# A gated block kernel's first mixer: position columns as a third group of the compression's product, and gelu, gate and clamps with one operand in PSUM

## The chip, the cores and the metric

The kernel runs on one core of one Trainium2 chip. The metric is the device time of one execution in microseconds (us). The core has a matrix engine (TensorE, in the rows PE, its weight loads PEld), a vector engine (VectorE, DVE), a scalar engine (ScalarE, ACT), GpSimd (POOL) and a queue that issues the DMAs (SyncE, SP). SBUF is the memory beside the engines; PSUM holds what the matrix engine writes and can be read and written by DVE and ACT.

## The reference, cut to what matters

Two blocks of two layers each are run over 256 tokens of width 1024. Each layer is a mixer and a gated feed-forward part. Only the first mixer is touched here. It projects the normed input and runs a retention of four heads and a sparse attention with three branches beside each other:

```python
proj = (h @ w_in).astype(jnp.float32)
(rq, rk, rv, rg, nq, kc, vc, ks, vs, kw, vw, ng) = _split(proj, EVEN_SIZES)
...
o_r = retention_chunkwise(q_r, k_r, heads(rv, RET_HEADS))
mu = jnp.mean(o_r, axis=-1, keepdims=True)
var = jnp.mean(jnp.square(o_r - mu), axis=-1, keepdims=True)
o_r = (o_r - mu) * lax.rsqrt(var + 1e-5)
o_r = ... * jax.nn.silu(rg)                      # the retention's gate
...
k_cmp = nsa_compress(kvh(kc), pos_k, w1_k, w2_k)  # and the same for v
...
def nsa_compress(kv, pos_emb, w1, w2):
    # 15 blocks of 32 tokens with a step of 16, two groups
    flat = (blocks + pos_emb.astype(jnp.float32)).reshape(B, G, n, CMP_BLOCK * d)
    return jax.nn.gelu(flat @ w1.astype(jnp.float32)) @ w2.astype(jnp.float32)
```

Since `(blocks + pos) @ w1 = blocks @ w1 + pos @ w1`, the kernel takes the product of the positions by itself, as one column that is the same for every block, and adds it. The attention's compressed branch has only 15 keys; its softmax keeps rows without a valid key at zero with small clamps.

## The kernel before

**Units.** All large products are a stream of weight chunks of up to 128x1024 elements. SP loads a chunk into `raw`, ACT rounds it into `whi` (line 1913, `split`), POOL takes the rest into `wlo` (line 2180, `lo`), and TensorE multiplies: for each 128 rows of weights the two products with `whi` (lines 1037 and 1038) and one with `wlo` (line 1044). Six chunks can be ahead: chunk c is rounded once chunk c-6 is used up. One chunk for one half of the tokens (t = 0 or 1) is a unit (`product`). The first mixer has units 0 to 69: seven blocks of projection columns (block 2 is 280 wide with units 16 to 21, the others 512 wide with eight units; the last, block 6, is the retention's gate and ends with unit 53), and from unit 54 on the output projection, whose units alternate t = 0, 1 up to 61. A block's product lies in `G[0]`, 512 columns for each t; `evict` (EV) copies it to `PJ0` with the norm's scale.

**Steps.** Everything else is small steps, each named by two letters and a key, and the order on every engine is written out by hand in `PLAN`: line "18:" lists the steps that come after unit 18, and each engine takes from it those that are its own, in that order. Engines are in order, so a step that waits holds everything behind it on its engine. Steps wait for each other by semaphores counted by `nth`.

**The compression.** TT turns the keys and values, TC (ACT, lines 2005 and 2006) copies them into `Z`, one plane of 256 columns for each of two groups, the lower 64 rows shifted by a token. CA (TensorE) then makes 16 matmuls over 30 columns (two groups of 15 blocks, line 1113), and 16 with one column, the positions held in `CP` (line 1117), with the same weights `w1c`. In the rows each such matmul of 32-bit floats stands as two. CB (DVE) copies the position's column to SBUF, adds it and makes the argument of gelu's exponential; CE (ACT) is the exponential; CD (DVE) finishes gelu; CF (TensorE) is the second product and CG (DVE) copies it to `CK`.

**The attention.** For branch br (0 compressed, 1 selected, 2 window), group g and half t: SC scores (TensorE, line 1146), MK mask and maximum (DVE), EX exponentials (ACT), TR turned weights (TensorE, line 1182), CPA and CPV their copies (ACT, DVE), AV weighted values (TensorE, line 1211), NO gated sum into `MX` (DVE). They work in three lanes: `@0` and `@1` are PSUM tiles A0 and A1, `@2` is `G[1]`; a lane's next user waits until the one before has finished.

**The retention's gate.** R1 to R7 make the retention's heads, their mean and the inverse deviation, in lane 2 (heads 0 and 1, key 0) and lane 0 (heads 2 and 3, key 1). After EV 6 t, GS (DVE, line 1683) clamps the negated gate from `PJ0` into the compression's old weights `w1c`, GT (ACT, lines 1902, 1904 and 1906) makes its sigmoid there, GU (DVE, line 1689) multiplies it into the gate in `PJ0`, and R8 (DVE, lines 1667 and 1675) normalises four 128x128 pieces in PSUM and writes their product with the gate to `MX`. MT 2 (TensorE, line 1080) turns key 0 of it, MH and ML (ACT, DVE) round it, MT 3 does so for key 1; the output projection needs MH/ML 2 from unit 62 and MH/ML 3 from unit 64 on.

## Time and profile before

| | |
|---|---|
| median of 3 runs | 1376.7 us (1375.18 to 1377.59) |
| the profiled execution's own time | 1377.06 us |
| its span, first to last instruction | 1375.3 us |
| TensorE busy | 1330.7 us, 97% of the span |
| POOL, ACT, DVE busy | 1033.3, 717.1 and 383.5 us |
| mean granted TensorE clock | 0.984 of full |

The profile is of one execution. Its own time lies 0.36 us over the median and 1.8 us over its span. Busy time of an engine says little by itself: what matters is which waits lie on the chain of work that ended last. Matmuls are pipelined, so the durations of neighbours overlap; the starts tell the pace. A granted clock of 1.00 is 2.4 GHz and 0.50 is 1.2 GHz.

### The profile page before, as it was taken

How to read it: one execution, taken by the hardware profiler on the slowest of the kernel's cores; microseconds unless marked ns; L12 is line 12 of the kernel's file. 1: busy time of each engine (PE TensorE's matmuls, PEld its weight loads, DVE VectorE, ACT ScalarE, POOL GpSimd, SP SyncE). 2: the span in 40 equal slices, each digit the busy share in tenths (PEclk: the TensorE clock that was granted, in tenths of full speed). 3: DMA queues.
4: the chain of work that ended last, by engine and by line, in shares of the span. 5: the costliest groups of instructions: out<-in, count | busy, mean ns of one | idle time of the engine just before them, and what ended most of it. 6: DMA issues, size and time to landing. Idle time of an engine off the chain costs nothing.

```text
span 1375.3 us, 19563 instructions
## 1 busy us (share of the span) xinstructions
PE 1330.7 (97%) x7558; PEld 1095.0 (80%) x7558; DVE 383.5 (28%) x812; ACT 717.1 (52%) x1259; POOL 1033.3 (75%) x875
## 2 busy tenths in 40 slices
PE   6999999999999999999999998999999999999997
PEld 4888788888878777888887777788887788788886
DVE  1155421111157653110104463301103232411112
ACT  6355564454478776544444664444534554544431
POOL 6354878887885467888888776788879877788874
PEclk9799999999999999999999999999999999999999
DMA  8232456665644244666665643566656545466652
GB/s 272 92 108 77 138 172 184 188 196 172 193 158 124 79 123 128 201 190 183 180 191 158 184 125 122 154 214 186 196 173 209 182 140 153 139 214 187 197 170 89
DMA packets 63117, 224.92 MB, mean 164 GB/s; under 512 B 7345, under 2 KB 7985, under 8 KB 63025
## 3 DMA queue, kind: packets, MB, share of 16 engines
q1 hardware_dynamic: 62736, 223.57, 53.2%
q8 instruction: 60, 0.98, 0.3%
q14 instruction: 33, 0.26, 0.1%
q10 hardware_dynamic: 288, 0.10, 0.0%
HBM read 222.59 MB, written 1.05 MB: 163 GB/s over the span
## 4 chain that ended last, share of the span: by engine, by line
PE 88%; DVE 3%; POOL 3%; ACT 3%; DMA 2%; issue 2%; DVEq 0%; SPq 0%; ACTq 0%
PE G L1037 25%; PE G L1044 25%; PE G L1038 25%; POOL wlo L2180 3%; PE A L1211 2%; PE A L1068 1%; ACT whi L1913 1%; PE A L1146 1%; PE G L1211 1%; PE A L1182 1%; PE A L1058 1%; PE A L1080 1%; DMA raw<-in_w_e 0%; DMA raw<-in_w_a 0%; PE A L1320 0%
## 5 line engine op out<-in xcount | busy, mean ns | idle before, releaser
L2180 POOL TENSOR_TENSOR wlo<-raw,whi 128x256 fp32r<-128x256 f32 (+1 forms) x867 | 1023.7, 1218 | 324.0 <-ACT whi L1913 323.9
L1913 ACT ACTIVATE whi<-raw 128x1024 fp32r<-128x1024 f32 x403 | 425.1, 1060 | 357.3 <-PE G L1044 334.4
L1037 PE MATMUL G<-whi,xh 128*128 128x512 f32 (+2 forms) x1200 | 464.9, 391 | 9.2 <-DVE xl L1392 6.8
L1038 PE MATMUL G<-whi,xl 128*128 128x512 f32 (+2 forms) x1200 | 452.0, 380 | 0.0
L1044 PE MATMUL G<-wlo,xh 128*128 128x512 f32 (+2 forms) x1200 | 353.2, 380 | 1.3 <-POOL wlo L2180 1.3
L1037 PEld LDWEIGHTS G<-whi,xh 128*128 128x128 f32 x1200 | 228.3, 190 | 52.2 <-ACT whi L1913 7.6
L1038 PEld LDWEIGHTS G<-whi,xl 128*128 128x128 f32 x1200 | 228.6, 190 | 37.7
L1044 PEld LDWEIGHTS G<-wlo,xh 128*128 128x128 f32 x1200 | 219.9, 190 | 46.6 <-POOL wlo L2180 3.2
L1037 PE MATMUL G<-whi,hh 128*128 128x512 f32 x352 | 139.4, 396 | 0.0
L1038 PE MATMUL G<-whi,hl 128*128 128x512 f32 x352 | 138.8, 394 | 0.0
L1044 PE MATMUL G<-wlo,hh 128*128 128x512 f32 x352 | 110.4, 395 | 0.0
L1044 PEld LDWEIGHTS G<-wlo,hh 128*128 128x128 f32 x352 | 66.3, 188 | 15.4
L1038 PEld LDWEIGHTS G<-whi,hl 128*128 128x128 f32 x352 | 66.3, 188 | 15.1
L1037 PEld LDWEIGHTS G<-whi,hh 128*128 128x128 f32 x352 | 66.4, 189 | 15.0
L1431 DVE SCALAR_TENSOR_TENSOR sa<-G,SM,sa 128x512 f32<-128x512 f32 (+1 forms) x24 | 16.9, 706 | 165.5 <-PE G L1044 165.5
L1434 DVE TENSOR_TENSOR sa<-G,sa 128x512 f32<-128x512 f32 (+1 forms) x24 | 15.5, 646 | 169.7 <-PE G L1044 169.7
L1442 DVE TENSOR_TENSOR hl<-A,hh 128x512 fp32r<-128x512 f32 (+1 forms) x48 | 31.1, 647 | 96.0 <-ACT hh L1982 96.0
L1037 PE MATMUL G<-whi,mh 128*128 128x512 f32 x128 | 53.5, 418 | 2.4 <-DVE ml L1449 1.5
L1038 PE MATMUL G<-whi,ml 128*128 128x512 f32 x128 | 51.6, 403 | 0.0
L1375 DVE SCALAR_TENSOR_TENSOR G<-X,G 128x512 f32<-128x512 f32 x16 | 11.1, 696 | 119.3 <-PE G L1044 119.3
L1375 DVE SCALAR_TENSOR_TENSOR X<-X,G 128x512 f32<-128x512 f32 x16 | 11.0, 687 | 114.8 <-PE G L1044 114.8
L1044 PE MATMUL G<-wlo,mh 128*128 128x512 f32 x128 | 41.5, 406 | 0.0
(340 smaller groups left out, 1196.7 us busy)
## 6 DMA issues: line engine op xcount, KB each, us to landing
raw<-in_g SPq DMA_DIRECT2D x88, 512.0 KB, 3.9
raw<-in_u SPq DMA_DIRECT2D x88, 512.0 KB, 4.0
raw<-in_d SPq DMA_DIRECT2D x88, 512.0 KB, 4.2
raw<-in_w_h SPq DMA_DIRECT2D x32, 512.0 KB, 3.6
raw<-in_w_e SPq DMA_DIRECT2D x24, 512.0 KB, 3.7
raw<-in_w_a SPq DMA_DIRECT2D x24, 512.0 KB, 3.6
raw<-in_w_b SPq DMA_DIRECT2D x24, 512.0 KB, 3.8
raw<-in_w_eo SPq DMA_DIRECT2D x8, 512.0 KB, 3.6
```

The costliest lines, as they stand in the source:

```text
L1037: e.matmul(o, sh[:, kt, xs], whi[h][:, ws], start=u.first and j == 0, stop=False)
L1038: e.matmul(o, sl[:, kt, xs], whi[h][:, ws], start=False, stop=False)
L1044: m = e.matmul(o, sh[:, kt, xs], wlo[h][:, ws], start=False, stop=u.stop and final)
L1058: m = e.transpose(A[t][:, 512 * b + 128 * i:512 * b + 128 * i + 128], X[:, t, 512 * b + 128 * i:512 * b + 128 * i + 128], ident)
L1068: m = e.transpose(A[t][:, 512 * (b % 2) + 128 * i:512 * (b % 2) + 128 * i + 128], sa[b % 2][:, t, 128 * i:128 * i + 128], ident)
L1211: m = e.matmul(tile[:, ow * i:ow * i + ow], w[1][0:kp, at:at + 128], vs[i][b], start=b == 0, stop=b == nb - 1)
L1375: e.scalar_tensor_tensor(out=x if st < 4 else ps, in0=x, scalar=1.0 if st < 4 else ALPHA, in1=ps, op0=ALU.mult, op1=ALU.add).then_inc(S["R ...
L1431: e.scalar_tensor_tensor(out=s_, in0=ps, scalar=rstd[st - 1, t], in1=s_, op0=ALU.mult, op1=ALU.mult).then_inc(S["HM"], 1)
L1434: e.tensor_tensor(s_, ps, s_, ALU.mult).then_inc(S["HM"], 1)
L1442: e.tensor_tensor(hl[sl], ps, hh[sl].bitcast(F), ALU.subtract).then_inc(S["HL"], 1)
L1913: e.activation(whi[c % NH][:, 0:n], raw[c % NR][:, 0:n], ACT.Copy).then_inc(s_hi, 1)
L2180: m = e.tensor_tensor(wlo[c % NH][:, i:j], raw[c % NR][:, i:j], whi[c % NH][:, i:j].bitcast(F), ALU.subtract)
```

## The change

It has five parts. (1) `Z` has a third plane for each of keys and values; MB, at the start, clears it and copies the 16 position columns into its even places, and CA becomes 16 matmuls over 45 columns (30 in use before, now three groups of 15); the 16 one-column matmuls are gone, and column 30 of the result is the position's. (2) Gelu's intermediates u and v lie in the lane's PSUM tile. (3) GS reads the gate's product from `G[0]` with the norm's scale instead of the evicted copy; TensorE's first unit of the output projection for each t now waits for GS as well as EV, since it writes `G[0]`. GU is gone; R8 makes two products over 512 columns, heads by sigmoid in PSUM and that by the gate in `PJ0` into `MX`. (4) The compressed branch's mask, maximum and clamps, NO's clamp and the copy in R6 are done in PSUM or left out. (5) The plan's lines 17 to 47 and 53 to 57 are in another order. Parts of the diff that repeat these are left out.

```diff
-17: TC 0; SC 1 0 0 @2; TC 1; CA 0 @0; MK 1 0 0; EX 1 0 0; CA 1 @1; CB 0; CE 0; TR 1 0 0; CD 0
-18: CPA 1 0 0; CB 1; CF 0; EV 2 0; AV 1 0 0; CG 0; CE 1
-19: CD 1; CF 1; SC 1 0 1 @0; CG 1; SC 0 0 0 @1; MK 1 0 1
+17: TC 0; SC 1 0 0 @2; TC 1; CA 0 @0; MK 1 0 0; EX 1 0 0; CA 1 @1; CB 0; CE 0; CD 0; TR 1 0 0
+18: CB 1; CPA 1 0 0; CF 0; EV 2 0; AV 1 0 0; CG 0; CE 1; SC 1 0 1 @0; CD 1; CF 1
+19: MK 1 0 1
+20: CG 1; SC 0 0 0 @1; EX 1 0 1
 21: MK 0 0 0
-22: EV 2 1; EX 1 0 1; GD
-24: GE; EX 0 0 0; TR 1 0 1; NO 1 0 0
-25: CPA 1 0 1; CPV 1 0 1; TT 3 @2; RO 0 0; AV 1 0 1; TC 3; SC 2 0 0 @2; NO 1 0 1; TR 0 0 0
...
+30: EX 0 0 1; TR 2 0 1; NO 2 0 0
+31: CPV 2 0 1; CPA 2 0 1; TR 0 0 1; SC 1 1 0 @2; AV 2 0 1; CPA 0 0 1; MK 1 1 0; EX 1 1 0; AV 0 0 1; NO 2 0 1
+32: NO 0 0 1; TR 1 1 0; SC 1 1 1 @0; CPA 1 1 0; MT 0 @1; MK 1 1 1; AV 1 1 0; MH 0
...
+40: NO 0 1 0; R1 0 @2
+41: MK 0 1 1; R2A 0; R2V 0; EX 0 1 1; R1 1 @0; R3 0; R2V 1; EV 5 0; TR 0 1 1; R2A 1; R4 0
+42: CPA 0 1 1; AV 0 1 1; R3 1; NO 0 1 1
+43: R4 1; MT 1 @1
...
+46: EV 5 1; R5 0; R5 1; R6 0
+47: R6 1; R7 0
 48: R7 1
 50: EV 6 0; GS 0
 51: GT 0
-53: GU 0
-54: EV 6 1
-55: GS 1; GT 1
-57: GU 1; R8 0; R8 1; MT 2 @1
+54: EV 6 1; GS 1
+55: GT 1
+56: R8 0
+57: R8 1; MT 2 @1
...
-        Z = sb("Z", [128, 4, 256], F, e0)
+        Z = sb("Z", [128, 6, 256], F, e0)
...
@@ -1025,6 +1026,8 @@
                         e.wait_ge(S["EV"], nth("EV", u.st, u.blk - 1, u.t))
                     elif u.st % 2 == 0 and wide and u.bank == 0:
                         e.wait_ge(S["EV"], nth("EV", u.st, len(BLOCKS[u.st]) - 1, u.t))
+                        if u.st == 0:
+                            e.wait_ge(S["GS"], nth("GS", 0, u.t))
...
-                e.wait_ge(d_cp, 16)
+                e.wait_ge(S["MB"], nth("MB", 0))
                 for m in range(16):
-                    z = Z[:, 2 * kind:2 * kind + 2, 2 * m:2 * m + 225:16]
+                    z = Z[:, 3 * kind:3 * kind + 3, 2 * m:2 * m + 225:16]
                     wt = w1c[:, kind, 64 * m:64 * m + 64]
-                    e.matmul(tile[0:64, 0:30].rearrange("p (g i) -> p g i", g=2), wt, z, start=m == 0, stop=m == 15)
-                for m in range(16):
-                    wt = w1c[:, kind, 64 * m:64 * m + 64]
-                    pos = CP[:, (POSV if kind else POSK) + m:(POSV if kind else POSK) + m + 1]
-                    o = e.matmul(tile[0:64, 512:513], wt, pos, start=m == 0, stop=m == 15)
+                    o = e.matmul(tile[0:64, 0:45].rearrange("p (g i) -> p g i", g=3), wt, z, start=m == 0, stop=m == 15)
                 o.then_inc(S["CA"], 1)
...
-                x, u, bias = w[0][0:64, 0:30], w[0][0:64, 32:62], w[0][0:64, 96:97]
+                x, u, bias = w[0][0:64, 0:30], tile[0:64, 64:94], w[0][0:64, 96:97]
                 k = -2.0 * (2.0 / np.pi) ** 0.5
                 e.wait_ge(S["CA"], nth("CA", *key))
-                e.tensor_copy(bias, tile[0:64, 512:513]).then_inc(s_dve, dv.up())
...
-                _, w = lane_of("CA", key)
-                x, u, v = w[0][0:64, 0:30], w[0][0:64, 32:62], w[0][0:64, 64:94]
+                tile, w = lane_of("CA", key)
+                x, u, v = w[0][0:64, 0:30], tile[0:64, 64:94], tile[0:64, 96:126]
                 e.wait_ge(S["CE"], nth("CE", *key))
                 e.tensor_scalar(u, u, 1.0, None, ALU.add).then_inc(s_dve, dv.up())
                 own()
                 e.reciprocal(v, u).then_inc(s_dve, dv.up())
                 own()
-                e.tensor_tensor(x, x, v, ALU.mult).then_inc(S["CD"], 1)
...
+                else:
+                    e.wait_ge(d_cp, 16)
+                    e.memset(Z[:, 2:6:3, :], 0.0).then_inc(s_dve, dv.up())
+                    own()
+                    for kind, at_pos in enumerate((POSK, POSV)):
+                        e.tensor_copy(Z[:, 3 * kind + 2, 0:32:2], CP[:, at_pos:at_pos + 16])
                 e.tensor_copy(one[:, :], ident)
                 e.tensor_copy(under[:, :], CN[:, at + 128:at + 256]).then_inc(S["MB"], 1)
...
                     e.wait_ge(d_cn, 16)
-                    mask = CN[:, C_CMP + 16 * t:C_CMP + 16 * t + nk].unsqueeze(1).to_broadcast([128, 2, nk])
-                    for b in range(2):
-                        m = e.tensor_tensor(s[:, b:4:2, :], heads4(tile[:, 512 * b:512 * b + 512], 2)[:, :, 0:nk], mask,
-                                            ALU.add)
-                    m.then_inc(s_dve, dv.up())
+                    mask = CN[:, C_CMP + 16 * t:C_CMP + 16 * t + nk].unsqueeze(1).to_broadcast([128, 4, nk])
+                    four = tile[:, :].rearrange("p (b k) -> p b k", b=4)[:, :, 0:nk]
+                    top = tile[:, 128:132]
+                    e.tensor_tensor(four, four, mask, ALU.add).then_inc(s_dve, dv.up())
                     own()
-                    e.tensor_reduce(mx[key], s, X_AX, ALU.max).then_inc(s_dve, dv.up())
+                    e.tensor_reduce(top.rearrange("p (i b) -> p b i", b=2),
+                                    tile[:, :].rearrange("p (b i k) -> p b i k", b=2, i=2)[:, :, :, 0:nk], X_AX, ALU.max,
+                                    ).then_inc(s_dve, dv.up())
                     own()
-                    e.tensor_scalar(mx[key], mx[key], -1.0e20, -1.0, ALU.max, ALU.mult).then_inc(S["MK"], 1)
+                    e.tensor_scalar(mx[key], top, -1.0e20, -1.0, ALU.max, ALU.mult).then_inc(S["MK"], 1)
...
+                    e.tensor_scalar(over, sm[key], 1.0e-30, None, ALU.max).then_inc(s_dve, dv.up())
                     own()
-                e.reciprocal(over, sm[key]).then_inc(s_dve, dv.up())
+                e.reciprocal(over, over if br == 0 else sm[key]).then_inc(s_dve, dv.up())
...
-                m.then_inc(s_dve, dv.up())
-                own()
-                e.tensor_copy(ret_va[hp], mv[:, 1:8:2]).then_inc(S["R6"], 1)
+                m.then_inc(S["R6"], 1)
...
+                heads = tile[:, :].rearrange("p (i b) -> p i b", i=2)[:, :, 0:256].rearrange("p i (t c) -> p i t c", t=2)
+                gate = w1c[:, :, 256 * hp:256 * hp + 256].rearrange("p t (i c) -> p i t c", i=2)
+                raw_gate = PJ0[:, :, RG + 256 * hp:RG + 256 * hp + 256].rearrange("p t (i c) -> p i t c", i=2)
+                to = MX[:, :, 512 + 256 * hp:768 + 256 * hp].rearrange("p t (i c) -> p i t c", i=2)
...
                 for t in range(2):
-                    e.wait_ge(S["GU"], nth("GU", 0, t))
-                for j in range(4):
-                    c, t, o = 128 * (2 * hp + j // 2), j % 2, 512 * (j // 2) + 128 * (j % 2)
-                    m = e.tensor_tensor(MX[:, t, 512 + c:640 + c], tile[:, o:o + 128],
-                                        PJ0[:, t, RG + c:RG + c + 128], ALU.mult)
-                m.then_inc(S["R8"], 1)
+                    e.wait_ge(S["GT"], nth("GT", 0, t))
+                    e.wait_ge(S["EV"], nth("EV", 0, 6, t))
+                e.tensor_tensor(heads, heads, gate, ALU.mult).then_inc(s_dve, dv.up())
+                own()
+                e.tensor_tensor(to, heads, raw_gate, ALU.mult).then_inc(S["R8"], 1)
 
             def ret_gate_clamp(key):
                 _, t = key
                 e.wait_ge(S["CA"], 2)
                 e.wait_ge(S["EV"], nth("EV", 0, 6, t))
-                e.tensor_scalar(w1c[:, t, 0:512], PJ0[:, t, RG:RG + 512], -1.0, 80.0, ALU.mult,
-                                ALU.min).then_inc(S["GS"], 1)
-
-            def ret_gate_silu(key):
-                _, t = key
-                e.wait_ge(S["GT"], nth("GT", *key))
-                e.tensor_tensor(PJ0[:, t, RG:RG + 512], PJ0[:, t, RG:RG + 512], w1c[:, t, 0:512],
-                                ALU.mult).then_inc(S["GU"], 1)
+                e.tensor_scalar(w1c[:, t, 0:512], G[0][:, 512 * t:512 * t + 512], rstd[-1, t], -80.0, ALU.mult,
+                                ALU.max).then_inc(S["GS"], 1)
...
+            def sigmoid_of_clamped(ap, done, sign=1.0):
+
+                e.activation(ap, ap, ACT.Exp, scale=sign).then_inc(s_act, ac.up())
...
-                        e.activation(Z[0:64, 2 * k + g, :], src, ACT.Copy)
-                        m = e.activation(Z[64:128, 2 * k + g, 0:255], src[:, 1:256], ACT.Copy)
+                        e.activation(Z[0:64, 3 * k + g, :], src, ACT.Copy)
+                        m = e.activation(Z[64:128, 3 * k + g, 0:255], src[:, 1:256], ACT.Copy)
...
-                _, w = lane_of("CA", key)
-                u = w[0][0:64, 32:62]
+                tile, _ = lane_of("CA", key)
+                u = tile[0:64, 64:94]
...
-                    m = e.activation(ps if key[0] == 4 else s[:, i, :], s[:, i, :] if key[:2] == (0, 0) else ps, ACT.Exp,
+                    m = e.activation(ps if key[0] == 4 else s[:, i, :], ps, ACT.Exp,
...
-                rstd_of(ret_r[hp], ret_va[hp], 1, 1.0, S["R7"])
+                rstd_of(ret_r[hp], ret_mv[hp][:, 1:8:2], 1, 1.0, S["R7"])
...
-                sigmoid_of_clamped(w1c[:, key[1], 0:512], S["GT"])
+                sigmoid_of_clamped(w1c[:, key[1], 0:512], S["GT"], -1.0)
```

## Rows read from the trace of the kernel before

**Rows 1.** Page, parts 1, 2 and 4: busy time, granted clock, chain that ended last.

```profile
PE 1330.7 (97%) x7558; PEld 1095.0 (80%) x7558; DVE 383.5 (28%) x812; ACT 717.1 (52%) x1259; POOL 1033.3 (75%) x875
...
PEclk9799999999999999999999999999999999999999
...
PE 88%; DVE 3%; POOL 3%; ACT 3%; DMA 2%; issue 2%; DVEq 0%; SPq 0%; ACTq 0%
```

**Rows 2.** Busy time by window: busy us per engine (instructions), then granted clock, DMA share, GB/s.

```profile
49.18:54.50 5.32, 5.32 (x93) 5.32 (x92) 1.81 (x7) 2.55 (x12) 2.12 (x4) 1.00 0.63 200
...
54.86:58.41 3.55, 3.55 (x36) 3.54 (x35) 0.53 (x3) 0.00 (x0) 0.00 (x0) 0.50 0.00 0
58.41:68.25 9.84, 9.84 (x44) 8.38 (x45) 2.22 (x11) 2.26 (x4) 1.49 (x3) 0.50 0.01 2
...
70.88:154.88 84.00, 84.00 (x530) 70.15 (x528) 42.76 (x120) 47.91 (x136) 43.41 (x62) 1.00 0.32 95
```

**Rows 3.** Chain of waits through the compression: start, us, what.

```profile
49.25 1.99 PE A L1113 x32
51.24 1.84 PE A L1117 x32
...
55.11 3.37 PE A L1117 x32
58.48 1.04 PE G L1182 x4
```

**Rows 4.** The same chain, one weight row of an output unit, at either clock.

```profile
166.64 0.83 PE G L1044 x2
...
168.83 0.47 PE G L1044 x2
```

**Rows 5.** Timeline around gelu's argument and first scores, DVE.

```profile
53.11 0.15 DVE L1457 COPY W<-A 64x1 f32<-64x1 f32 x1 [3.12 <-PE A L1117]
...
55.27 0.18 DVE L1478 TENSOR_TENSOR W<-W 64x30 f32<-64x30 f32 x1
```

**Rows 6.** Timeline, ACT, end of the first exponentials.

```profile
51.50 0.21 ACT L2028 ACTIVATION_READ_ACCUMULATOR W<-G,SM 128x1 f32 x1
```

**Rows 7.** Timeline of DVE through the retention's gate.

```profile
148.93 0.43 DVE L1683 TENSOR_SCALAR w1c<-PJ 128x512 f32<-128x512 f32 x1 [3.47 <-ACT PJ L1926]
...
155.87 1.03 DVE L1683 TENSOR_SCALAR w1c<-PJ 128x512 f32<-128x512 f32 x1 [2.61 <-ACT PJ L1926]
158.93 1.22 DVE L1689 TENSOR_TENSOR PJ<-PJ,w1c 128x512 f32<-128x512 f32 x1 [2.02 <-ACT w1c L1906]
160.07 1.37 DVE L1667 TENSOR_SCALAR G<-G,SM 128x128 f32<-128x128 f32 x4
```

**Rows 8.** Timeline of ACT there.

```profile
155.09 0.67 ACT L1926 ACTIVATE PJ<-G,SM 128x512 f32<-128x512 f32 x1
...
158.26 0.63 ACT L1906 ACTIVATE w1c<-w1c 128x512 f32<-128x512 f32 x1
```

**Rows 9.** Timeline of PE there, idle time before in brackets.

```profile
155.81 0.50 PE L1037 MATMUL G<-whi,mh 128*128 128x512 f32 x1 [0.93 <-ACT PJ L1926]
...
162.50 0.63 PE L1080 MATMUL A<-CN,MX 128*128 128x128 f32 x4 [2.23 <-DVE MX L1675]
```

**Rows 10.** Busy time by window around that wait, and at other short waits or short matmuls.

```profile
163.90:167.30 3.40, 3.40 (x10) 2.51 (x9) 1.26 (x5) 0.00 (x0) 3.40 (x6) 0.50 0.62 190
...
1175.50:1179.00 3.50, 1.27 (x8) 0.92 (x7) 3.38 (x7) 2.04 (x4) 3.50 (x6) 1.00 0.54 154
1179.00:1182.00 3.00, 3.00 (x18) 2.34 (x16) 2.79 (x5) 0.38 (x1) 3.00 (x5) 1.00 0.72 194
...
466.68:470.20 3.52, 3.52 (x168) 2.89 (x167) 2.85 (x8) 1.58 (x4) 0.00 (x0) 1.00 0.36 136
```

**Rows 11.** DVE groups by form, 28 to 180 us: us in total, mean ns.

```profile
L1449 DVE TENSOR_TENSOR ml<-A,mh 128x512 fp32r<-128x512 f32 x4 | 2.7, 686 | 4.9 <-ACT mh L1988 4.9
```

**Rows 12.** Timeline of POOL from 150 us on.

```profile
150.58 17.73 POOL L2180 TENSOR_TENSOR wlo<-raw,whi 128x256 fp32r<-128x256 f32 x24 [5.25 <-ACT whi L1913]
```

More of the change, by code:

```diff
@@ L289 @@
-44: MH 1; R2V 1
-45: ML 1; R3 1; EV 5 1; R5 0; R4 1
-46: R6 0; R5 1; R7 0
-47: R6 1
+23: EV 2 1; EX 0 0 0; GD; TR 1 0 1; GE
+24: CPV 1 0 1; CPA 1 0 1; NO 1 0 0; AV 1 0 1; TT 3 @2; NO 1 0 1; TR 0 0 0; TC 3
+25: CPA 0 0 0; SC 2 0 0 @2; RO 0 0; SC 2 0 1 @0; AV 0 0 0; MK 2 0 0
+26: MK 2 0 1; EX 2 0 0
+27: NO 0 0 0; TR 2 0 0
+28: SC 0 0 1 @1; CPA 2 0 0
+29: MK 0 0 1; EX 2 0 1; AV 2 0 0; RO 0 1
+30: EX 0 0 1; TR 2 0 1; NO 2 0 0
+31: CPV 2 0 1; CPA 2 0 1; TR 0 0 1; SC 1 1 0 @2; AV 2 0 1; CPA 0 0 1; MK 1 1 0; EX 1 1 0; AV 0 0 1; NO 2 0 1
@@ L293 @@
+42: CPA 0 1 1; AV 0 1 1; R3 1; NO 0 1 1
+43: R4 1; MT 1 @1
+44: MH 1
+45: ML 1
+46: EV 5 1; R5 0; R5 1; R6 0
+47: R6 1; R7 0
 48: R7 1
@@ L843, in program @@
         ret_st, ret_mv = [small(24) for _ in range(2)], [small(8) for _ in range(2)]
-        ret_va, ret_r = [small(4) for _ in range(2)], [small(4) for _ in range(2)]
+        ret_r = [small(4) for _ in range(2)]
         out_ms, out_r = [small(4) for _ in range(4)], [small(4) for _ in range(4)]
@@ L1477, in gelu_done @@
                 own()
-                e.tensor_tensor(x, x, v, ALU.mult).then_inc(S["CD"], 1)
+                e.tensor_tensor(x, v, x, ALU.mult).then_inc(S["CD"], 1)
             def compress_copy(key):
@@ L1898, in rstd_of @@
                 e.activation(to, to, ACT.Exp, scale=-0.5).then_inc(done, 1)
-            def sigmoid_of_clamped(ap, done):
-                e.activation(ap, ap, ACT.Exp).then_inc(s_act, ac.up())
+            def sigmoid_of_clamped(ap, done, sign=1.0):
+                e.activation(ap, ap, ACT.Exp, scale=sign).then_inc(s_act, ac.up())
                 own()
```

30 lines of the change are left out of this document (9 added, 21 removed), and 2 rows, old and new, of the table SIGNALS.

## The prediction

> **What bounds the kernel now.** I read the page first. TensorE is busy for 97% of the span and carries 88% of the chain that ended last, so time is to be had only where TensorE does less, stands, or runs at the lower clock. The line of the granted clock is full but for a few slices; one of them, with a 7, lies where the touched mixer begins [rows 1]. Next I cut the mixer into windows at the starts that the chain names. Through the compression TensorE never stands, yet between 54.50 and 54.86 us its clock falls to 0.50 and stays there to 68.25 us; from 70.88 to 154.88 us it is busy without a gap at the full clock [rows 2]. The chain names the work of the slow stretch: the compression's matmuls, both sets of positions among them [rows 3]. Last I read the timelines at the mixer's end. There TensorE stands twice, 0.93 us for EV 6 1 and 2.23 us for R8 [rows 9], and 3.40 us at the lower clock follow [rows 10]. What is saved in these three places arrives at the end of the kernel, as long as TensorE stays what all others wait for.
>
> **The position columns.** The 64 one-column instructions of line 1117 go: 1.84 us for the first 32 and 3.37 us for the second 32, which ran at half clock [rows 3]. Together 5.2 us of TensorE's own time, with nothing of another engine beside it that would keep TensorE waiting: the first exponentials are done at 51.71 us [rows 6], before TR 1 0 0 asks for them at about 53.1 (49.25 plus two groups of 1.9). The other 64 instructions grow from 30 to 45 columns. At the same clock 32 instructions of 30 columns took 1.99 us and 32 of one column 1.84 us, so 29 columns more cost 0.15 us and 15 more cost about 0.08 us for 32, 0.16 us for 64 [rows 3]. From above, two 512-column instructions take 0.47 us, 0.46 ns a column, which gives 0.44 us for 64 times 15 columns [rows 4]. I take 0.1, the near row is of the same shape.
>
> **The clock behind them.** The clock fell after 5.3 us of these short matmuls in a row, TensorE fully busy the whole time. It was not idleness that preceded it, it was instructions that stream one or 30 columns and mostly load weights [rows 2, 3]. After the change the row of them is 64 instructions, 3.8 us, each with more columns, and then come turned weights and a unit of 280 columns. I expect the clock to hold. From 58.48 to 68.25 us TensorE did 9.8 us of work at half clock [rows 2, 3]. The same two instructions take 0.83 us at half and 0.47 us at full clock [rows 4], those of line 1117 3.37 and 1.84 [rows 3], a ratio of 1.8. At full clock 9.8 us become 5.3 us: 4.5 us saved. If the clock falls all the same, this term is 0, or about 1.7 us if it falls for a shorter stretch. What speaks for its holding: 3.5 us with 168 short matmuls elsewhere ran at 1.00, and so did the units behind a window in which TensorE was busy for 1.27 of 3.50 us [rows 10].
> A rule points the other way. The Trainium skill, "TensorE: Matmul & The Clock Gate", section "What's actually happening", puts the lower clock down to the array having been idle, and the higher one to its having been busy for a while. By that rule alone a stretch in which TensorE was busy throughout could not bring the clock down, the fall behind 54.50 us would have another cause that the change leaves in place, and the sum would be smaller by the whole clock term. This trace does not agree with the rule read so narrowly, since the fall came with TensorE busy for 5.32 of 5.32 us [rows 2].
>
> **Gelu in PSUM, the third plane, the clamps.** CB 0 to CD 0 took from 53.11 to 55.45 us [rows 5]. It now starts at about 51.2 and ends near 53.7 with PSUM operands; CF 0 is asked for at about 54.3, after TR 1 0 0 (half of the 1.04 us that it took at half clock [rows 3]) and the six matmuls of unit 18, some 0.8 us. CF 1 comes behind AV 1 0 0 and SC 1 0 1, 2.4 us of TensorE, and its chain is done before. So gelu costs nothing; without that cover it would be 2.4 us. MB's added clearing and two copies lie on DVE before 30 us, and DVE's next work is at 49 us; nothing. The compressed branch's smaller steps save DVE some tenths, off the chain: nothing either way. TensorE has no gap in 84 us there [rows 2], so a faster DVE gives it nothing, and only a later one can cost.
>
> **The order of steps 17 to 47.** I followed TensorE's queue through the new lines. The closest places are SC 1 0 1 behind CG 0, which waits behind CB 1 on DVE, and MT 1 behind NO 0 1 1 and R4 0; behind a late step stand the next units. Each comes out within some tenths of being ready. I take 0.3 us of new waits; from below 0, since there is no gap to remove, and from above 3 us, one DVE step of 1.0 to 1.4 us, as those of [rows 7], at two or three places.
>
> **The gate, added wait.** Unit 55 waits for EV 6 1 now and starts at 155.81 [rows 9]. After the change it waits for GS 1 too. GS reads PSUM: the nearest row of 128x512 with a PSUM operand is 686 ns [rows 11], with some 0.1 us to start. Price 0.8 us (0.5 to 1.2: GS itself took 0.43 and 1.03 us from SBUF [rows 7]). Behind unit 55 stand all of TensorE's later work. What is late next is not GS but ACT: EV 6 1 came 0.93 us after TensorE wanted it, and that stays.
>
> **The gate, removed wait.** R8 was late by a chain that starts with GS 1 at 155.87: 1.03 us, three ACT steps to 158.89, GU 1.22, four pieces 1.37, the product [rows 7, 8]. Now GS ends about 156.6, the sigmoid 1.99 us later at 158.6; the four pieces no longer stand behind GU and are done before; two products of 512 columns at 0.69 [rows 11] and a little between make R8 0 ready near 160.1. TensorE comes to MT 2 at 160.27 plus the 0.8 us above, 161.1, so the 2.23 us [rows 9] go entirely. If both products took 1.22 us each, as GU did beside POOL [rows 7], R8 would be ready at 161.1, just in time. R8 1 follows with 1.4 and twice 0.7 us, near 163, and MT 3 wants it at 164.2.
>
> **The clock behind that wait.** 0.93 and 2.23 us of standing preceded the lower clock of 163.90 to 167.30 [rows 9, 10]. With one wait of 1.7 us left it should hold: 3.40 us become 1.85, 1.6 us saved, or 0 if not. POOL, which works without a pause for 17.7 us from 150.58 on [rows 12], has the last chunk of the output projection ready at 168.3; TensorE will want it at about 171.5, so POOL does not become the bound.
>
> **Sum.** -5.2 - 4.5 + 0.1 + 0.3 + 0.8 - 2.2 - 1.6 = -12.3 us. The profiled execution took 1377.06 us, 0.36 over the median of the runs shown; 1376.7 - 12.3 = 1364.4, and I say 1364.5. The rest of the kernel is as before and moves earlier as a block. There the clock also falls behind some short waits, and a shift can take such a fall away or add one, 1.6 us each.
>
> **Rivals.**
> 1. The clock falls in the compression after all, in part or whole, and perhaps again behind the wait of 1.7 us. For it: the 3.8 us are still mostly weight loads, and the cause is read from one place; against it the rows named. Gain 12.3 - 4.5 = 7.8, with the second fall 6.2: 1368.9 to 1370.5; a short fall only, 1366.
> 2. New waits of 1 to 3 us in the order of steps, and up to 0.4 for the columns: 1366 to 1368. For it: DVE is busy for half of the 84 us [rows 2] and TensorE reaches each step sooner than before in the first 10 us. Against it: the same engines fed TensorE without a gap.
> 3. More than the sum: a later fall of the clock goes too, or the order saves something: 1360 to 1362.5.
> 4. Slower, the other side: the new order makes TensorE wait at its steps in units 17 to 47. There are about 49 such steps; with 0.25 us at each the gain of 12.3 is used up, with 0.35 us the sum is +17 - 12.3, about 1381. For it only that the order is new; against it 84 us without a gap before.
> 5. No effect: POOL or the DMAs set the pace and the saving is waited away. POOL is busy 43.4 of 84 us there [rows 2]; 1376.7.
>
> **Chances.** The sum within its own range (1362.5 to 1366) 0.58; rival 1 0.17; rival 2 0.10; rival 3 0.08; rival 4 0.03; rival 5 0.04. The predicted time is that of the sum. The range 1360.8 to 1370.0 takes in rival 3 nearly whole, rival 2 and most of rival 1, and leaves out a bit over 1 in 10. A change within 0.2% (2.8 us) is about what a measurement of this kernel cannot tell from none; all of the sum and rivals 1 to 3 lie beyond it. Faster 0.93, same 0.04, slower 0.03.
>
> **What would show it.** Line 1117's matmuls gone, line 1113's group at 1.9 to 2.1 us for 32; granted clock 1.00 from 49 to 70 us; the first 512-wide unit of block 3 (unit 22) near 61.2 instead of 70.88 us; no new gaps to the end of unit 53; a wait of about 1.7 us for GS before unit 55; no wait before MT 2, and full clock behind it. Wrong would be a clock of 0.50 anywhere in the first mixer after 38 us, a gap before an SC, CF or MT, or a wait on POOL's `wlo` from 165 us on.

## The result and the profile after

The changed kernel takes 1368.69 us (median of 5, 1363.84 to 1370.22) beside 1375.18 us for the kernel before on the same chip: ratio 0.9943, 95% interval 0.992 to 0.9966. In a second comparison the medians were 1366.54 and 1374.06 us, ratio 0.9946 (0.9928 to 0.9965). Faster, by intervals that leave out 1, and inside the stated range; but the gain is 6.5 to 7.5 us where the sum said 12.3. The profiled execution took 1368.69 us, its span is 1366.9 us.

The page of the kernel after: busy time, granted clock in 40 slices, and the chain that ended last. They answer to [rows 1].

```profile
PE 1322.2 (97%) x7494; PEld 1087.1 (80%) x7494; DVE 383.3 (28%) x803; ACT 716.8 (52%) x1259; POOL 1032.0 (76%) x875
...
PEclk9999999999999999999999999999999999999999
...
PE 88%; DVE 3%; ACT 3%; DMA 2%; issue 2%; POOL 1%; SPq 0%; DVEq 0%; ACTq 0%
```

There are 64 matmul instructions fewer and 8.5 us less of busy TensorE, and the 7 in the second slice is a 9. TensorE's share of the chain is still 88%: it sets the pace as before.

The windows of the kernel after: compression, what follows it, the attention, then two around the gate (columns as in [rows 2]).

```profile
47.30:52.50 5.20, 5.20 (x67) 5.09 (x65) 2.56 (x10) 2.65 (x12) 2.13 (x4) 1.00 0.66 202
52.50:55.50 3.00, 3.00 (x25) 2.59 (x24) 2.06 (x10) 1.17 (x3) 0.00 (x0) 1.00 0.01 5
60.77:144.00 83.23, 82.77 (x523) 68.83 (x522) 41.07 (x114) 44.82 (x128) 42.79 (x63) 1.00 0.32 96
147.90:151.30 3.40, 3.40 (x9) 2.61 (x9) 2.43 (x7) 2.44 (x4) 3.40 (x6) 0.51 0.61 178
151.30:165.00 13.70, 13.70 (x64) 11.19 (x64) 4.61 (x9) 4.38 (x6) 12.54 (x18) 1.00 0.61 187
```

The clock holds at 1.00 through the compression, where [rows 2] had 0.50 for 13 us. It does not hold behind the gate's wait (0.51), where the prediction had it hold. In the attention and the retention (units 22 to 53) TensorE is 82.77 of 83.23 us busy: a small gap is new.

The chain through the compression, to be laid beside [rows 3]. Line 1116 is the product, 1181 the turned weights, 1145 the scores.

```profile
47.36 5.19 PE A L1116 x64
52.55 0.58 PE G L1181 x4
...
55.50 1.06 PE A L1145 x8
...
59.41 0.55 PE A L1145 x8
```

64 instructions of 45 columns take 5.19 us, 81 ns each. At 30 columns 32 took 1.99, 62 ns each [rows 3]. So 15 columns more cost 1.2 us, not 0.1, and more than the upper bound of 0.44.

TensorE's timeline, with the wait before each in brackets: the new gap, the first unit of the output projection for t = 0 and for t = 1 (unit 55), and MT 2. It answers to [rows 9]. The gap stands before line 1247, the retention's step R5 0, which waits for EV 5 1.

```profile
131.98 0.46 PE L1247 MATMUL G<-PJ,W 128*128 128x128 f32 x2 [0.46 <-ACT PJ L1928]
...
144.29 0.40 PE L1040 MATMUL G<-whi,mh 128*128 128x512 f32 x1
...
147.73 0.57 PE L1040 MATMUL G<-whi,mh 128*128 128x512 f32 x1 [1.88 <-DVE w1c L1689]
...
153.55 0.60 PE L1083 MATMUL A<-CN,MX 128*128 128x128 f32 x4
```

DVE's timeline through the gate, to be laid beside [rows 7]: GS 1, and R8's two products of 512 columns for key 0.

```profile
146.83 0.75 DVE L1689 TENSOR_SCALAR w1c<-G,SM 128x512 f32<-128x512 f32 x1 [6.18 <-ACT PJ L1928]
...
149.80 0.70 DVE L1681 TENSOR_TENSOR G<-G,w1c 128x512 f32<-128x512 f32 x1 [0.94 <-ACT w1c L1908]
150.54 0.69 DVE L1683 TENSOR_TENSOR MX<-G,PJ 128x512 f32<-128x512 f32 x1
```

The wait for GS is 1.88 us (1.7 was forecast), GS 0.75 us, the products 0.70 and 0.69, and MT 2 starts without a wait. All that is as forecast; only the clock is not.

**Where the time went.** Three marks stand in every profile: the compression's first matmul, the first product of the output projection (unit 54), and the first turning of the next stage (the first `L1058 x4` or `L1061 x4` of the chain behind it).

| us | before | after |
|---|---|---|
| start of the compression | 49.25 | 47.36 |
| compression's products | 9.23 | 5.19 |
| from their end to unit 54 | 94.84 | 91.74 |
| unit 54 to the next stage | 22.95 | 21.45 |
| next stage to the end of the span | 1199.0 | 1201.2 |

The change works in the middle three rows: -4.04 - 3.10 - 1.50 = -8.64 us. The first row is a matter of the start-up: in 14 profiles of this study the compression starts between 45.02 and 49.25 us, and kernels with all of the change's code stand at both ends (46.31 and 49.04). The last row scatters likewise, from 1195.2 to 1202.1 us in the eleven profiles whose kernels have nothing added there, whatever else they change. The largest wait in it is one in the second block's attention, in the chain of the kernel after:

```profile
1092.77 7.29 DMA raw<-in_w_b
...
1101.21 0.49 ACT W L2039
1101.74 1.10 PE G L1210 x8
```

TensorE waits 2.69 us there for an ACT copy that stands in ACT's queue behind the rounding of a weight chunk that landed late. In the second profile of the same kernel the wait is 1.55 us and the span 5.0 us shorter. The profile before has no wait over 0.8 us at this place, its repetition has one of 2.27 us at 766.01. This is why one pair of spans (1375.3 and 1366.9) is no measure of a change of a few us here, and the marks are.

### The profile page after: what moved, and what is told of

The parts are those of the page before. It is cut to its first block, busy times and chain, and to the rows that moved or that the text cites. A ratio compares the mean times of both kernels' runs of the same rounds, so it can differ in the third digit from the quotient of the medians.

```text
span 1366.9 us, 19430 instructions
## 1 busy us (share of the span) xinstructions
PE 1322.2 (97%) x7494; PEld 1087.1 (80%) x7494; DVE 383.3 (28%) x803; ACT 716.8 (52%) x1259; POOL 1032.0 (76%) x875
## 4 chain that ended last, share of the span: by engine, by line
PE 88%; DVE 3%; ACT 3%; DMA 2%; issue 2%; POOL 1%; SPq 0%; DVEq 0%; ACTq 0%
PE G L1040 26%; PE G L1041 25%; PE G L1047 25%; PE A L1210 2%; PE A L1071 1%; POOL wlo L2182 1%; ACT whi L1915 1%; DMA raw<-in_w_e 1%; PE A L1145 1%; DMA raw<-in_w_b 1%; PE G L1210 1%; PE A L1181 1%; PE A L1061 1%; PE A L1343 1%; PE G L1145 0%
## 5 line engine op out<-in xcount | busy, mean ns | idle before, releaser
L1041 PEld LDWEIGHTS G<-whi,hl 128*128 128x128 f32 x352 | 66.4, 189 | 14.9
```

Of the source, the lines that this page charges most:

```text
L1041: e.matmul(o, sl[:, kt, xs], whi[h][:, ws], start=False, stop=False)
```

## The experiments

**The two kernels again.** `after_again` and `before_again` are the two kernels as they are.

> The changed kernel once more, nothing edited. Theory A (what the first mixer saves is the same in every execution, and what comes later in the kernel is chance): the first 512-wide unit of block 3 starts again near 60.8 us and the feed-forward part behind the first mixer 10 to 11 us before that of the kernel before; the 2.7 us wait for the copied weights and the late weight chunk in the fourth mixer near 1100 us do not come again, and the clock falls in other places there. The ratio to before is 0.992 to 0.996. Theory B (the change itself has made the fourth mixer late, by the phase in which its transfers meet): the wait of more than 2 us near 1100 us stands there again.

> The kernel before once more. If the lower clock behind the compression is of the kernel and not of one execution, it falls again within the compression, somewhere from 52 to 57 us, for about as long as before (10 to 14 us); the first unit of block 3 starts at 69 to 71 us. Lower clock behind other short waits comes at other places than in the first profile. If it was chance, the compression stays at 1.00 here.

`after_again`: 1366.54 us. The clock is 1.00 through the compression, the wait for GS is 1.88 us again and the clock falls behind it again. `before_again`: one run of 1376.24 us; the clock is 0.50 from 52.7 to 66.4 us (compression at 47.53), 3.4 us of low clock stand behind the gate's waits, unit 54 to the next stage is 22.94 us. Both patterns repeat. The gain on the marks does not repeat to the same size: from the compression's start to the next stage `before_again` takes 126.99 us (127.02 in the first profile) and `after_again` 120.04 (118.38), so 6.95 us instead of 8.64. The difference is new low clock in `after_again`, seen in two windows around 88 us:

```profile
83.90:87.80 3.90, 3.90 (x36) 3.48 (x34) 1.42 (x4) 2.09 (x9) 2.18 (x4) 1.00 0.69 175
88.20:91.50 3.30, 3.30 (x12) 2.48 (x10) 1.46 (x6) 0.09 (x1) 0.00 (x0) 0.50 0.20 79
```

TensorE is busy throughout and the clock falls all the same, behind 3.6 us of products of 128 and 64 columns (scores, weighted values). It costs 1.6 us: from the compression's end to unit 54 the changed kernel takes 91.74 us without such a fall and 93.37 with it. So the two gains on the marks, 8.64 and 6.95 us, lie around the 7.5 us of the larger comparison.

**The third group alone.** The kernel before, with the third plane of Z and the 45-column product; nothing else of the change. The edit in short:

```diff
-    16 matmuls of tile[0:64, 0:30]  from Z[:, 2 * kind:2 * kind + 2, ...]
-    16 matmuls of tile[0:64, 512:513] from CP
+    16 matmuls of tile[0:64, 0:45]  from Z[:, 3 * kind:3 * kind + 3, ...]
```

> The kernel before with the position columns alone: third plane, 16 matmuls over 45 columns, the one-column matmuls gone; gelu, gate, clamps and the order of steps as before. Theory A (the matmuls and the clock behind them carry the change): the 64 instructions take 5.2 us at full clock, no lower clock between 49 and 70 us, the first unit of block 3 starts 9 to 10 us before 70.88 us, and the 2.2 us wait before MT 2 with 3.4 us of lower clock behind it stays; ratio 0.9935 to 0.996, the same as the whole change within its interval. Rival (the order of steps carries it): the first unit of block 3 starts less than 7 us earlier, or new waits of TensorE over 1 us show before unit 54.

1366.42 us, ratio 0.9949 (0.993 to 0.9968): the whole of the measured gain. The clock is 1.00 from the compression's start at 46.56; its end is at 51.75, unit 54 at 142.20, 90.45 us later, against 91.74 in the changed kernel. So gate, gelu, clamps and order together bring nothing that the medians show. On the marks they bring 0.24 us (118.62 us from the compression's start to the next stage, against 118.38): 1.5 us are won at the gate, and the stretch before it has become 1.3 us longer. The gate's waits are as in [rows 9], in TensorE's timeline:

```profile
144.69 0.50 PE L1037 MATMUL G<-whi,mh 128*128 128x512 f32 x1 [0.93 <-ACT PJ L1928]
...
151.38 0.63 PE L1080 MATMUL A<-CN,MX 128*128 128x128 f32 x4 [2.22 <-DVE MX L1677]
```

**The positions back.** The changed kernel with the one-column matmuls in place of the third group. The edit in short:

```diff
-    16 matmuls of tile[0:64, 0:45]
+    16 matmuls of tile[0:64, 0:30]
+    16 matmuls of tile[0:64, 512:513] from CP
```

> The changed kernel with the two times 16 one-column matmuls back in place of the third group; all else of the change stays. If the one-column matmuls bring the clock down: 30-column instructions at 60 ns, the one-column ones at 58 ns, a clock of 0.50 from about 5 us behind the compression's start, and the first unit of block 3 near 69 us instead of 60.8. If not the one-column matmuls but chance did it: the clock stays at 1.00 and that unit starts near 63.5 us.

One run of 1368.97 us. The chain through the compression:

```profile
45.02 1.99 PE A L1116 x32
47.01 1.84 PE A L1120 x32
48.84 3.25 PE A L1116 x32
52.09 3.37 PE A L1120 x32
```

The windows of its second 3.5 us and its third:

```profile
48.50:52.00 3.50, 3.50 (x39) 3.50 (x39) 1.87 (x9) 0.17 (x1) 0.00 (x0) 0.57 0.34 133
52.00:55.50 3.50, 3.50 (x34) 3.49 (x34) 0.01 (x1) 0.00 (x0) 0.00 (x0) 0.50 0.00 0
```

The fall is back with the one-column matmuls. It comes here some 4 us after the compression's start, not 5.4 as in the first profile of the kernel before. From the compression's start to unit 54 it is 105.58 us, against 96.93 in the changed kernel. These 8.65 us are the place of the gain. The single time says little of it, because in its profile the compression starts 2.3 us earlier, and the way from the next stage to the end is the shortest of all, 1195.2 us.

**Is it the length of the row of short matmuls?** Each product is issued twice, 128 instructions of 45 columns in a row. The edit in short:

```diff
     for m in range(16): ... o = e.matmul(tile[0:64, 0:45] ...)
+    for m in range(16): ... o = e.matmul(tile[0:64, 0:45] ...)
```

> The changed kernel with each of the two compression products issued twice (128 instructions of 45 columns and as many weight loads in a row instead of 64; the first half's sums are overwritten with the same values). Theory A (a long row of short matmuls brings the clock down, whatever they are): the clock falls to 0.50 inside or right behind the row, 5 to 10 us after its start, as with 30 and one column, and unit 22 starts some 10 us later than in the changed kernel. Rival B (it is the one-column instructions): the clock is 1.00 throughout, the row takes 10.4 us (128 x 81 ns) instead of 5.2, and unit 22 starts 5.2 us later.

One run of 1372.83 us. The windows of the row, in halves, and behind it:

```profile
49.04:54.20 5.16, 5.16 (x66) 5.16 (x67) 0.69 (x1) 2.42 (x11) 2.06 (x3) 1.00 0.66 206
54.20:59.30 5.10, 5.10 (x66) 4.99 (x65) 1.87 (x9) 0.17 (x1) 0.00 (x0) 1.00 0.00 0
59.30:70.00 10.70, 10.70 (x77) 9.22 (x78) 4.09 (x15) 6.13 (x15) 3.83 (x6) 1.00 0.01 3
```

The row takes 10.25 us, all at 1.00: rival B. The length of the row alone is not it.

**Rows of other widths, elsewhere.** Behind unit 62 the pattern of the kernel before (32 of 30 columns, 32 of one, twice), behind unit 66 128 of 30. The edit in short:

```diff
+    for n in {62: (30, 1, 30, 1), 66: (30, 30, 30, 30), 70: (1, 1, 1, 1)}[u]:
+        16 matmuls of n columns into A[1][0:64, 512:512 + n]
```

> The changed kernel with three added rows of 128 short products each (the compression's weights, results that nothing reads): behind unit 62 the pattern of the kernel before (32 of 30 columns, 32 of one, twice), behind unit 66 128 of 30 columns, behind unit 70 128 of one column. Theory A (one-column products bring TensorE's clock down, wherever they stand): 0.50 inside or right behind the first and the third row, 1.00 through the second; the three rows take 7.7, 8.0 and 7.4 us at full clock. Rival B (30 columns do it too, 45 are enough to hold it): also behind the second. Rival C (it has to do with the place, the compression beside its transfers, not with the columns): 1.00 through all three.

The stage has no unit 70, so the third row was not issued. One run of 1384.16 us. Windows of the first row in halves, and of the second:

```profile
159.64:163.40 3.76, 3.76 (x67) 3.76 (x66) 0.00 (x0) 0.00 (x0) 3.76 (x6) 1.00 0.68 217
164.30:169.50 5.20, 5.20 (x52) 5.19 (x50) 0.00 (x0) 0.00 (x0) 0.00 (x0) 0.50 0.34 105
178.02:185.60 7.58, 7.58 (x130) 7.54 (x130) 0.95 (x4) 1.34 (x3) 2.78 (x4) 1.00 0.21 71
```

The mixed row falls at about 164.3, 4.7 us after its start, and 10.2 us at the lower clock follow; 128 of 30 columns hold. Rivals B and C are out, as far as one execution can say. The missing row was made good in a further kernel, here against this one:

```diff
-    {62: (30, 1, 30, 1), 66: (30, 30, 30, 30), 70: (1, 1, 1, 1)}
+    {62: (1,), 66: (1, 1, 1, 1)}
```

> The changed kernel with 32 added one-column products behind unit 62 and 128 of them behind unit 66 (results that nothing reads). The kernel with the mixed rows did not issue its row of one column alone, since the stage has no unit 70. Theory A (one column is enough by itself, and how many follow each other matters): 32 of them, 1.84 us, leave the clock at 1.00; in the row of 128 it falls to 0.50 some 2 to 5 us after the row's start, and the row takes 10 to 12 us instead of 7.4. Rival B (it is the change between 30 columns and one that brings the clock down): 1.00 through both rows, 1.84 and 7.4 us.

One run of 1382.99 us. Windows: the 32, what follows them, then start and rest of the 128.

```profile
161.38:163.30 1.92, 1.92 (x33) 1.91 (x33) 0.00 (x0) 0.00 (x0) 1.92 (x4) 1.00 0.48 190
163.30:167.50 4.20, 4.20 (x19) 3.41 (x19) 0.69 (x1) 0.42 (x1) 1.88 (x3) 1.00 0.68 198
169.55:172.00 2.45, 2.45 (x43) 2.45 (x44) 0.94 (x4) 1.33 (x3) 1.04 (x2) 1.00 0.03 7
173.50:180.40 6.90, 6.90 (x66) 6.90 (x65) 0.00 (x0) 0.00 (x0) 0.23 (x1) 0.50 0.25 76
```

The 32 of one column leave the clock alone. The 128 bring it down some 3.3 us after they begin, it stays down for 13.7 us, and the row takes 10.95 us. That is theory A as it was put. How few columns it takes, between one and 30, no run shows.

**The price of a column.** Rows of 32 instructions with the compression's weights behind units 62 to 67, in words:

```diff
+    62: 30 columns, 2 groups   63: 45, 3 groups    64: 45 adjacent
+    65: 60 columns, 4 groups   66: 36 adjacent     67: 60 adjacent
+    (within a group every 16th float of Z)
```

> The changed kernel with six added rows of 16 products each (32 instructions, the compression's weights, results that nothing reads) behind units 62 to 67: 30 columns in 2 groups of stride 16, 45 in 3 groups of stride 16, 45 adjacent, 60 in 4 groups of stride 16, 36 adjacent, 60 adjacent. Theory A (the time goes with the columns): per instruction about 60 ns at 30, 81 at both of 45, 100 or more at both of 60, 67 at 36. Rival B (the stride or the number of groups sets the price): 45 and 60 adjacent columns take about 60 ns like 30, those in groups 81 and 100. Rival C (the floor is that of the weight load, and 81 ns come from what stands beside it in the compression): 60 ns for all but the widest.

One run of 1379.62 us. The chain through the six rows, in that order:

```profile
162.15 1.99 PE A L1124 x32
...
165.73 2.66 PE A L1126 x32
...
169.98 1.99 PE A L1128 x32
...
173.57 3.45 PE A L1130 x32
...
179.01 1.99 PE A L1132 x32
...
182.97 2.01 PE A L1134 x32
```

62, 83, 62, 108, 62 and 63 ns per instruction: rival B. Up to 60 adjacent columns cost no more than 30. Columns 64 bytes apart cost 1.8 ns each (83/45 and 108/60), once that is more than a floor of about 60 ns, under which 30 of them hide. That the floor is the weight load's is likely, since each instruction has one, but no run shows it. The wider rows here also have more groups; the last kernel below tells the two apart. The estimate of 0.1 us had read two points, 1 and 30 columns, that both lie on the floor.

**The old order.** The changed kernel with the plan's lines 17 to 47 of the kernel before.

```diff
...
-18: CB 1; CPA 1 0 0; CF 0; EV 2 0; AV 1 0 0; CG 0; CE 1; SC 1 0 1 @0; CD 1; CF 1
+18: CPA 1 0 0; CB 1; CF 0; EV 2 0; AV 1 0 0; CG 0; CE 1
...
```

> The changed kernel with the steps of units 17 to 47 in the order of the kernel before; the steps of the gate stay as changed. Theory A (the new order costs TensorE time although it shows no wait): the start of MH 0 comes 82.4 us after the start of unit 22, as in both kernels that have the old order, against 83.5 to 83.6 us with the new one, and the time is 0.5 to 1.5 us under the changed kernel's (ratio to it about 0.999). Rival B (the 1.1 us are a fall of the clock or a profile's own scatter, or belong to the gelu or the branch steps): still 83.5 us, and the changed kernel's time. The clock is 1.00 through the compression in both.

1365.13 us, ratio 0.9951 (0.9932 to 0.997); the changed kernel was not in this comparison, and its ratios of 0.9943 and 0.9946 cannot be told from that. The profile can: unit 54 comes 90.45 us behind the compression (142.98 less 52.53), to the hundredth as in the third group alone, against 91.74. The gap of 0.46 us is gone: from the compression to unit 54 TensorE has no idle time at all. The score steps SC 1 0 1 and SC 0 0 0 follow each other again:

```profile
57.15 1.41 PE A L1144 x16
```

In the kernel after they stand apart, at 1.06 and 0.55 us, 0.20 us more together. So theory A: the new order costs 1.3 us. 0.46 of it is the wait. The other 0.8 us are no idle time: the same number of instructions stand in the stretch, and their starts lie further apart (added up, the 88 of the scores take 0.40 us more, 0.20 of that in the two steps shown, and the 128 of the weighted values 0.23). (The expectation counted from unit 22; counted from the compression's end the comparison is cleaner.)

A second price is likely, but not shown. In the middle of the attention the clock fell in 4 of 8 profiles with the new order (at 87, 88, 116 and 122 us), and in none of 6 with the old. Each of the four falls comes within 0.9 us of the end of one of two rows of 32 short products that only the new order puts together, 3.6 and 3.4 us long. The chain of `after_again` shows the first of them:

```profile
84.32 0.65 PE G L1145 x8
84.97 2.96 PE A L1210 x24
```

The last eight of the 24 are the compressed branch's, whose weights fill only 15 of the 128 rows. The old order's longest rows are 3.35 and 2.86 us, without such products. Which of this matters, length or rows, was not tested; the 10.25 us of 45 columns at 1.00 say that neither a long row nor few columns is enough by itself.

**The gate from SBUF.** GS clamps the evicted copy, as in the kernel before, and TensorE does not wait for it. The edit in short:

```diff
-    if u.st == 0: e.wait_ge(S["GS"], nth("GS", 0, u.t))
-    e.tensor_scalar(w1c[...], G[0][...], rstd[-1, t], -80.0, ALU.mult, ...)
+    e.tensor_scalar(w1c[...], PJ0[:, t, RG:RG + 512], 1.0, -80.0, ALU.mult, ...)
```

> The changed kernel, but GS clamps the copy that EV 6 has put into PJ0 (factor 1.0) instead of PSUM, and TensorE's wait for GS ahead of unit 55 is gone. Theory A (the wait of 1.88 us behind EV 6 1 and GS 1 costs 0.95 us and lets the clock fall, 1.6 us more): TensorE waits 0.93 us for EV 6 1 alone ahead of unit 55, the clock stays at 1.00 from 140 to 170 us, R8 0 is ready before MT 2 asks for it, and the time is about 2.5 us below the changed kernel's. Rival B (any wait of some 0.9 us there brings the clock down, or MT 2 waits again because it comes 1 us earlier): 0.50 for 3.4 us all the same, and a gain of 1 us or less.

1367.65 us, ratio 0.9954 (0.9938 to 0.997), no gain over the changed kernel by the medians. TensorE's timeline and the windows, the second from unit 55 to the next stage:

```profile
148.74 0.50 PE L1038 MATMUL G<-whi,mh 128*128 128x512 f32 x1 [0.93 <-ACT PJ L1926]
...
153.18 0.63 PE L1081 MATMUL A<-CN,MX 128*128 128x128 f32 x4
```

```profile
116.40:120.00 3.60, 3.60 (x15) 3.08 (x14) 1.48 (x6) 0.50 (x2) 0.00 (x0) 0.54 0.03 14
148.74:165.00 16.26, 16.26 (x73) 13.02 (x74) 7.92 (x16) 7.19 (x10) 16.26 (x24) 1.00 0.53 177
```

At the gate all is as theory A said: 0.93 us of wait, the clock holds, MT 2 does not wait, and unit 54 to the next stage is 19.19 us against 21.45. That is 2.26 us: 0.95 of the wait, and 1.3 of the low clock behind it. 1.6 us were lost again in this profile 30 us earlier, at 116, to a fall of the kind that the new order has. What is left, 0.6 us on the marks (117.79 against 118.38), a comparison of medians cannot tell: its interval reaches 2.2 us to either side. Against the third group alone, the gate edit without the wait for GS is worth 3.8 us here (22.98 less 19.19).

**Both, and then adjacent columns.** Old order and gate from SBUF; then the same with Z sorted, so that the 15 windows of a group are adjacent.

> The changed kernel with the old order of the steps of units 17 to 47, and with GS reading the copy in PJ0 so that TensorE does not wait for it. Theory A (the two costs are separate and add): MH 0's first product 90.45 us behind the end of the compression's products (91.7 with the new order), next stage's first transpose about 19.2 us behind that, as in the kernel with the gate from SBUF alone (21.3 with the wait for GS), so it starts near 162.2 us; a wait of 0.93 us ahead of unit 55, the clock at 1.00 from 52 to 165 us. Some 3 us below the changed kernel, 1363 us. Rival B (something takes the gain back, a new fall of the clock or the late weight chunk in the fourth mixer): the transpose at 162.2, the end within 1 us of the kernel with the old order alone.

The edit against the first of them; the position columns are laid out to match:

```diff
-    z = Z[:, 3 * kind:3 * kind + 3, 2 * m:2 * m + 225:16]
+    z = Z[:, 3 * kind:3 * kind + 3, 16 * (m % 8) + m // 8:16 * (m % 8) + m // 8 + 15]
...
-    e.activation(Z[0:64, 3 * k + g, :], src, ACT.Copy)
-    m = e.activation(Z[64:128, 3 * k + g, 0:255], src[:, 1:256], ACT.Copy)
+    for half in range(2):   # pairs = src as (q r e) -> r q e
+        m = e.activation(Z[64 * half:64 * half + 64, 3 * k + g, 0:128] ..., pairs[:, :, :, half], ACT.Copy)
```

> As the kernel with the old order and the gate from SBUF, and Z holds the even positions sorted so that the 15 windows of a group are adjacent columns (the copies out of PSUM write 128 columns instead of 256). Theory A (columns 64 bytes apart are what makes 45 columns cost 81 to 83 ns, 62 adjacent): the compression's 64 instructions take 4.0 instead of 5.2 us, the three groups still being apart, and the end comes 1.2 us earlier, about 1362 us. Rival B (the jumps between the three groups cost as well, or the copies into Z get slow and TensorE waits for TC): 5.2 us as before, or a wait ahead of CA 0.

The first takes 1361.84 us, ratio 0.9907 (0.9883 to 0.993), the second 1361.66 us, ratio 0.9904 (0.9885 to 0.9922). The two windows of the first kernel, and then chain and windows of the second:

```profile
46.70:144.00 97.30, 97.20 (x658) 82.45 (x658) 46.73 (x139) 52.90 (x152) 48.40 (x71) 1.00 0.29 94
144.82:162.00 17.18, 17.18 (x79) 13.78 (x80) 8.36 (x17) 7.72 (x11) 17.18 (x25) 1.00 0.59 186
```

```profile
46.79 3.86 PE A L1113 x64
```

```profile
46.79:143.00 96.21, 95.87 (x659) 81.17 (x658) 46.67 (x139) 52.32 (x151) 48.63 (x71) 1.00 0.30 96
143.59:161.00 17.41, 17.41 (x80) 13.97 (x81) 8.60 (x17) 7.96 (x12) 17.27 (x25) 1.00 0.59 190
```

In the first the two savings add: 90.45 us to unit 54, 19.19 us to the next stage, full clock throughout, the next stage at 161.53 us (165.74 in the changed kernel). In the second the 64 instructions take 3.86 instead of 5.19 us, 60 ns each, the jumps between groups cost nothing, the ACT copies take 272 instead of 379 ns, and the next stage starts at 160.29. The 1.2 us are plain in the profile and not in the medians. The ratios went from the changed kernel's 0.9943 and 0.9946 to 0.9907 and 0.9904, some 5 us, though they come from different comparisons and their intervals overlap at the ends. The marks are surer: from the compression's start to the next stage the two take 114.83 and 113.50 us, 3.6 and 4.9 us less than the changed kernel's better profile, and the first is 12.2 us under the kernel before, which is about the prediction's sum, though made up of other terms.

## Why the prediction was right, and what in it was wrong

The sign was right, and for the reason given: one-column matmuls go, and with them the low clock behind them. The size was off: 12.3 forecast, 8.64 and 6.95 measured on the marks, 6.5 and 7.5 by the medians. That 1368.69 us still lies inside 1360.8 to 1370.0 is owed to the room left for rivals 1 and 2; it lies outside the sum's own range of 1362.5 to 1366, which had a chance of 0.58. What came is a part of both: rival 1's second fall of the clock, behind the gate's wait, and rival 2 in small. By the sum's own terms, in the first pair of profiles:

| term | forecast | measured |
|---|---|---|
| columns' instructions, and the clock behind them | -9.7 | -9.6 |
| 30 to 45 columns | +0.1 | +1.2 |
| order of steps | +0.3 | +1.3 |
| GS wait for unit 55 | +0.8 | +0.95 |
| wait ahead of MT 2 | -2.2 | -2.2 |
| clock behind the gate's wait | -1.6 | -0.2 |
| sum | -12.3 | -8.55 |

The first line is from the third group alone: from the compression's start to unit 54 it needs 95.64 us, the kernel before 104.07, so -8.43, and with the 1.2 for the columns taken out -9.6. It was forecast in two halves, 5.2 for the instructions and 4.5 for the clock, and both fit: the compression's products take 5.24 us less beside the 1.2, and from their end to unit 54 it is 4.39 us less. The clock's -0.2 behind the gate is a difference: a fall of 3.4 us is there before and after, but it costs 1.5 us before (22.95 us less the wait of 2.23 and the 19.19 of the kernel with the gate from SBUF, which has neither that wait nor the fall) and 1.3 after (21.45 less 0.95 and 19.19). Why the same length costs less there is open.

**Clock in the compression: right.** It falls in each of three profiles with the one-column matmuls and in none of eleven with the third group. The reading that it was not idleness but the kind of instruction has been tested by itself, at another place, and held. It was half right in naming "one or 30 columns": 128 of 30 columns leave the clock at 1.00. The rule that the prediction had set against it, from the Trainium skill, "TensorE: Matmul & The Clock Gate", section "What's actually happening", puts the lower clock down to the array having been idle. Read by the profile's busy time the runs do not agree: TensorE was 6.90 of 6.90 us busy at 0.50 in the row of one column, and the fall went away with the one-column matmuls, so it had no other cause that the change left in place.

**Columns: mis-sized by 1.1 us.** The step that failed is "29 columns more cost 0.15 us and 15 more cost about 0.08 us for 32". Both ends, 58 and 62 ns, lay at the floor of some 60 ns per instruction, where the number of columns does not show, and the bound from above was taken from 512 adjacent columns. Neither row had more strided columns than hide under the floor.

**Order of steps: too low by 1.0 us.** 1.3 us, inside the bounds of 0 to 3. The one wait, 0.46 us, stands before R5 0 and not at the two places named as closest (SC 1 0 1 and MT 1). The 0.8 us that are no wait were not priced at all: TensorE takes longer over the same steps in another order.

**The gate: waits right, clock wrong, the largest error (1.4 us).** The wait is 1.88 us and GS takes 0.75; R8 0 is ready at 151.23, well ahead of MT 2 at 153.55. But "with one wait of 1.7 us left it should hold" was a guess, and it is the other step that failed outright: the clock was 0.51 for 3.4 us behind the wait. Of eight profiles with the wait of 1.88 us the clock fell behind it in six; behind the 0.93 us of the other six in none. The changed wait gave away 0.95 us and mostly 1.3 us more for an operand in PSUM that saved DVE nothing that anyone waited for: GS took 0.75 us from PSUM and 0.59 us from SBUF in `gate_sbuf`.

**The rest of the kernel: "moves earlier as a block", not so.** It scatters by 7 us between profiles with its own waits and falls of the clock, so single spans hide terms of 1 us.

One of the prediction's own signs of being wrong came, a clock of 0.50 in the first mixer, and so did a gap where it had said "no new gaps to the end of unit 53". They mark two of the three terms that were off.

## What to carry to other kernels

Price a TensorE instruction by what it streams and how that lies in memory: a price read between two points at the floor of an instruction says nothing of the slope above it, and sorting an operand once can make a wider product free. Count a product of one column at more than its own time: many in a row bring the clock down and everything behind them pays. And when a change bundles a large gain with small edits, try them alone: here the third group carried the gain, the new order and the wait for GS gave part of it back, and undoing those two made the best kernel.

## What the runs showed of the hardware that was not expected

- TensorE at 100% busy does not keep its clock: 128 one-column products brought it from 1.00 to 0.50 some 3.3 us after their start and held it there for 13.7 us, while 128 of 30 and of 45 columns ran 7.6 and 10.3 us at 1.00. Each is one execution.
- An instruction of these 32-bit matmuls with 64 columns of weights took 58 ns for one column and 60 to 63 ns for 30 to 60 adjacent ones; columns 64 bytes apart cost 1.8 ns each where that comes to more: 83 ns for 45, 108 ns for 60. With the 15 of a group adjacent, 45 columns take 60 ns.
- The same kernel at the same place can keep or lose the clock from run to run: behind the wait of 1.88 us (six of eight), and behind rows of 3.4 and 3.6 us of products of 15 to 128 columns (in four of eight profiles, behind one of the two).
